# Three units of each up projection taken in two halves of 128 rows

## What is computed

```python
# first block
h = rmsnorm(x, norm_gains[l, 2]) * (1.0 + sc2) + sh2
y = jnp.square(jax.nn.relu(h @ w1[l] + b1[l])) @ w2[l] + b2[l]     # w1: 1024 x 4096
x = x + g2 * rmsnorm(y, norm_gains[l, 3])
# second block
h = h + _swiglu(_rms_norm(h, norm_ffn_g[l]), w_ffn_in[l], w_ffn_out[l])   # w_ffn_in: 1024 x 5632
def _swiglu(x, w_in, w_out):
    g, u = jnp.split(x @ w_in, 2, axis=-1)
    return (jax.nn.silu(g) * u) @ w_out
```

## Time and profile before

| | |
|---|---|
| median of three runs | 787.77 us |
| the profiled execution | 789.94 us |
| its span, first to last instruction | 788.2 us |
| TensorE busy | 734.8 us, 93% |
| VectorE busy | 517.8 us, 66% |
| ScalarE busy | 450.2 us, 57% |
| mean granted clock of TensorE | 0.974 of full |

### The profile page before, as it was taken

One profiled execution on the slowest core, in us unless ns is written; L12 is line 12 of the kernel. 1 busy time (PEld: TensorE's weight loads), 2 busy tenths in 40 slices (PEclk: granted clock), 3 DMA queues, 4 the chain that ended last, 5 costly groups with the idle time before them and its releaser, 6 DMA issues.

```text
span 788.2 us, 12072 instructions
## 1 busy us (share of the span) xinstructions
PE 734.8 (93%) x4062; PEld 619.8 (79%) x4062; DVE 517.8 (66%) x764; ACT 450.2 (57%) x724; POOL 44.4 (6%) x77
## 2 busy tenths in 40 slices
PE   0599999789999999989999999999897999999998
PEld 0498966589999886767989777777686888888886
DVE  6877697777877643457657465665747777777443
ACT  1654678666666433355455687554446777777331
POOL 3100100100000100014101000000000000000000
PEclk9899999979999999998999999999997999999999
DMA  8999985257787655534763564544444666656661
GB/s 315 368 330 338 262 278 167 81 150 206 233 240 263 213 187 166 175 117 115 227 189 114 181 187 131 164 125 138 148 123 134 179 188 175 201 175 197 203 196 57
DMA packets 137167, 150.50 MB, mean 191 GB/s; under 512 B 6164, under 2 KB 111783, under 8 KB 137129
## 3 DMA queue, kind: packets, MB, share of 16 engines
q1 hardware_dynamic: 135278, 145.28, 59.9%
q10 hardware_dynamic: 1852, 4.75, 1.7%
HBM read 148.57 MB, written 1.44 MB: 190 GB/s over the span
## 4 chain that ended last, share of the span: by engine, by line
PE 80%; DVE 10%; issue 4%; ACT 3%; DMA 3%; POOL 1%; SPq 0%; POOLq 0%; DVEq 0%; ACTq 0%
PE acc L1363 13%; PE acc L1364 13%; PE acc L1365 13%; PE acc L1355 11%; PE acc L1342 6%; PE acc L1344 6%; PE acc L1343 6%; PE acc L1356 5%; DVE ada_sum L1038 3%; DMA raw<-in_w_ada 2%; PE aux L1331 2%; DVE wl L960 1%; DMA raw<-in_w_out 1%; PE acc L1595 1%; ACT wh L594 1%
## 5 line engine op out<-in xcount | busy, mean ns | idle before, releaser
L960 DVE TENSOR_TENSOR wl<-raw,wh 128x1024 fp32r<-128x1024 f32 x217 | 266.2, 1232 | 149.5 <-ACT wh L594 148.4
L594 ACT ACTIVATE wh<-raw 128x1024 fp32r<-128x1024 f32 x217 | 227.9, 1055 | 125.6 <-PE acc L1365 109.6
L1342 PE MATMUL acc<-xT,wh 128*128 128x256 f32 x440 | 126.9, 288 | 5.5 <-DVE xT L990 4.1
L1355 PE MATMUL acc<-xT,wh 128*128 128x512 f32 x352 | 127.0, 405 | 0.8 <-DVE xT L982 0.8
L1344 PE MATMUL acc<-xT,wl 128*128 128x256 f32 x440 | 126.1, 287 | 0.0
L1343 PE MATMUL acc<-xT,wh 128*128 128x256 f32 x440 | 126.1, 287 | 0.0
L1363 PE MATMUL acc<-wh,xT 128*128 128x512 f32 (+1 forms) x272 | 111.0, 408 | 4.7 <-DVE xT L982 2.6
L1364 PE MATMUL acc<-wl,xT 128*128 128x512 f32 (+1 forms) x272 | 106.5, 391 | 0.0
L1365 PE MATMUL acc<-wh,xT 128*128 128x512 f32 (+1 forms) x272 | 106.3, 391 | 0.0
L1356 PE MATMUL acc<-xT,wl 128*128 128x256 f32 x352 | 100.0, 284 | 0.0
L1342 PEld LDWEIGHTS acc<-xT,wh 128*128 128x128 f32 x440 | 85.9, 195 | 7.5 <-issue 5.9
(11 more groups left out here) (260 smaller groups left out, 877.1 us busy)
## 6 DMA issues: line engine op xcount, KB each, us to landing
raw<-in_w_in SPq DMA_DIRECT2D x66, 512.0 KB, 3.6
raw<-in_w SPq DMA_DIRECT2D x64, 512.0 KB, 3.8
raw<-in_w_ffn_in SPq DMA_DIRECT2D x44, 512.0 KB, 4.1
raw<-in_w_ada SPq DMA_DIRECT2D x27, 512.0 KB, 6.5
raw<-in_w_ffn_out SPq DMA_DIRECT2D x22, 512.0 KB, 4.3
raw_more<-in_w_ada SPq DMA_DIRECT2D x13, 512.0 KB, 7.2
raw<-in_w_out SPq DMA_DIRECT2D x13, 512.0 KB, 4.8
rows_tmp<-in_w_ada ACTq DMA_DIRECT2D x8, 512.0 KB
```

What stands on the lines that cost most here:

```text
L594: A(wh[:, s, :], raw_unit, ACT.Copy).then_inc(rounded, 1)
L960: V.tensor_tensor(wl[:, s, :], raw_slot(r), wh[:, s, :].bitcast(f32), ALU.subtract).then_inc(split_ready, 1)
L1342: mm(bank[:, 0:ROWS], wh[:, s, w], hi, start=(kt == 0), stop=False)
L1355: mm(bank[:, :], wh[:, s, w], moving[:, kt, :], start=(kt == 0), stop=False, skip_group_check=True)
```

## The change

In both up projections the first three units are no longer taken by the loop but written out in parts. A new function `row_part` multiplies one unit by one row tile (128 rows) for some of the kt. TensorE's new order in up 1: transposes of row tile 0; units 0 and 1 by row tile 0, kt 0 to 3; unit 0 by row tile 0, kt 4 to 7; transposes of row tile 1; unit 1 by row tile 0, kt 4 to 7; unit 2 by row tile 0; then units 0, 1 and 2 by row tile 1; then the fourth unit as before, and the loop from its second pass on, without waits for columns. In up 2 units 0 and 1 by row tile 0, kt 0 to 3 stand ahead of the transposes of row tile 1 and kt 4 to 7 of both behind them. In up 1 a part has three matmuls over 128 columns for each kt; in up 2 one over 256 (the high and the low part of 128 rows) and one over 128. ScalarE and VectorE get their steps in an order that fits.

```diff
@@ ScalarE, up 1
             square_rows(N_FF1, 1)
+            from_transposed(X_UP1, 0, range(4, KT), A2, sh2)
             round_static(U_UP1 + 2)
-            from_transposed(X_UP1, 0, range(4, KT), A2, sh2)
             from_transposed(X_UP1, 1, range(KT), A2, sh2)
@@ VectorE, up 1
             split_columns(X_UP1, 0, range(4), 4)
             low_static(U_UP1 + 1)
+            split_columns(X_UP1, 0, range(4, KT), 4)
             normalise(N_FF1, 1)
-            split_columns(X_UP1, 0, range(4, KT), 4)
+            low_static(U_UP1 + 2)
             split_columns(X_UP1, 1, range(KT), 2)
-            low_static(U_UP1 + 2)
@@ VectorE, up 2
             split_columns(X_UP2, 0, range(4), 4)
+            low_static(U_UP2 + 1)
             normalise(N_FF2, 1)
             split_columns(X_UP2, 0, range(4, KT), 4)
-            split_columns(X_UP2, 1, range(4), 2)
-            low_static(U_UP2 + 1)
-            split_columns(X_UP2, 1, range(4, KT), 2)
             low_static(U_UP2 + 2)
+            split_columns(X_UP2, 1, range(KT), 2)
@@ TensorE
+            def row_part(u, t, r, kts, bank, both):
+
+                s = slot_of(u)
+                pe.wait_ge(split_ready, u + 1)
+                for kt in kts:
+                    pe.wait_ge(xT_ready, X_COUNT * t + (4 * (kt // 4 + 1) if r == 0 else KT + 2 * (kt // 2) + 2))
+                    w, rows = slice(P * kt, P * (kt + 1)), slice(P * r, P * (r + 1))
+                    moving = xT[:, kt, :].rearrange("p (c n) -> p c n", c=2)[:, :, rows]
+                    first, last = kt == 0, kt == KT - 1
+                    if both:
+                        out = bank[:, :].rearrange("p (c n) -> p c n", c=2)[:, :, rows]
+                        mm(out, wh[:, s, w], moving, start=first, stop=False, skip_group_check=True)
+                    else:
+                        mm(bank[:, rows], wh[:, s, w], moving[:, 0, :], start=first, stop=False, skip_group_check=True)
+                        mm(bank[:, rows], wh[:, s, w], moving[:, 1, :], start=False, stop=False, skip_group_check=True)
+                    ins = mm(bank[:, rows], wl[:, s, w], moving[:, 0, :], start=False, stop=last, skip_group_check=True)
+                return ins
@@ TensorE, up 1
-            for r in range(RT):
-                to_columns(xr, r, X_UP1, normed, RT + r + 1)
-
+            to_columns(xr, 0, X_UP1, normed, RT + 1)
+            pe.wait_ge(resid, 1)
+            for k in range(2):
+                row_part(U_UP1 + k, X_UP1, 0, range(4), acc[k], False)
+            row_part(U_UP1, X_UP1, 0, range(4, KT), acc[0], False)
+            to_columns(xr, 1, X_UP1, normed, RT + 2)
+            row_part(U_UP1 + 1, X_UP1, 0, range(4, KT), acc[1], False)
             pe.wait_ge(resid, RT)
-            with pe.Fori(0, D_FF // P // RING) as i:
+            row_part(U_UP1 + 2, X_UP1, 0, range(KT), acc[2], False)
+            for k in range(3):
+                row_part(U_UP1 + k, X_UP1, 1, range(KT), acc[k], False).then_inc(unit_done, 1)
+            col_unit(U_UP1 + 3, U_UP1 + 4, acc[3], xT)
+            with pe.Fori(1, D_FF // P // RING) as i:
                 for k in range(RING):
                     pe.wait_ge(acc_free, F_PROJ1 - RING + k + 1 + RING * i)
-                    col_unit(U_UP1 + k, U_UP1 + k + 1 + RING * i, acc[k], xT, columns_ready(X_UP1) if k == 0 else None)
+                    col_unit(U_UP1 + k, U_UP1 + k + 1 + RING * i, acc[k], xT)
@@ TensorE, up 2
+            pe.wait_ge(resid, 2 * RT + 1)
+            for k in range(2):
+                row_part(U_UP2 + k, X_UP2, 0, range(4), acc[k], True)
             to_columns(xr, 1, X_UP2, normed, 3 * RT + 2)
+            for k in range(2):
+                row_part(U_UP2 + k, X_UP2, 0, range(4, KT), acc[k], True)
             pe.wait_ge(resid, 3 * RT)
-            with pe.Fori(0, FF2 // P // 2) as i:
+            row_part(U_UP2 + 2, X_UP2, 0, range(KT), acc[2], True)
+            for k in range(3):
+                row_part(U_UP2 + k, X_UP2, 1, range(KT), acc[k], True).then_inc(unit_done, 1)
+            both_unit(U_UP2 + 3, U_UP2 + 4, acc[3], xT)
+            with pe.Fori(1, FF2 // P // 2) as i:
```

More of the change, by code:

```diff
@@ L1749, in _ @@
             wide_rows(U_OUT2, lambda k: xT[:, k, :], range(KT - 1, KT), 1, None, KT - 1)
+            pe.wait_ge(resid, 2 * RT + 1)
+            for k in range(2):
+                row_part(U_UP2 + k, X_UP2, 0, range(4), acc[k], True)
             to_columns(xr, 1, X_UP2, normed, 3 * RT + 2)
+            for k in range(2):
+                row_part(U_UP2 + k, X_UP2, 0, range(4, KT), acc[k], True)
             pe.wait_ge(resid, 3 * RT)
-            with pe.Fori(0, FF2 // P // 2) as i:
+            row_part(U_UP2 + 2, X_UP2, 0, range(KT), acc[2], True)
[3 more added lines that the diff above has]
+            with pe.Fori(1, FF2 // P // 2) as i:
                 for k in range(RING):
                     pe.wait_ge(acc_free, F_PROJ2 - RING + k + 1 + RING * i)
-                    both_unit(U_UP2 + k, U_UP2 + k + 1 + RING * i, acc[k], xT, columns_ready(X_UP2) if k == 0 else None)
+                    both_unit(U_UP2 + k, U_UP2 + k + 1 + RING * i, acc[k], xT)
             n_hid = FF2 // P
```

## The result

The changed kernel takes 803.02 us (median of 8 runs) against 788.03 for the kernel before beside it (8 runs). The comparison gives a ratio of 1.0117, interval 1.0076 to 1.0158: slower by 1.2%. (The comparison leaves out the two longest executions, 805.97 and 805.28, as disturbed, but both belong to the upper of the two groups described next, so its ratio is too low; the quotient of the medians is 1.019.) The forecast was 805.7, with slower at 0.64.

The account below looks back on a forecast made before the run. TensorE, busy 93% of the span, was taken as the bound, with hand-over gaps carried whole to the end. Up 1 +18.4 and up 2 -0.5 gave +17.9: 807.8 profiled, 805.7 in the runs' terms, range 786 to 813.

Parts of the forecast that it names:

- The narrow matmul costs a whole one: Divided units: a matmul on 128 columns takes 0.112 us at full clock, 0.213 at low, paced by its weight load.
- The second rival: 128 columns cost half of 256, by the page's issue gap: up 1 -5.6, up 2 -5.8, total 776.4; chance 0.04.
- Up 1, +16.35 and +2.05: Up 1 at low clock throughout: fourth unit starts 16.35 us late, then loses 2.05 itself; sum +18.4.
- A clock that stays low through all 144: Up 1: the clock falls and does not rise under the 144 narrow matmuls; forecast case, chance 0.55.
- The first rival: The clock rises also under loads that fill the time: up 1 +2.9, up 2 -2.4, total 788.3; chance 0.33.
- The transposes in the middle: Rival: row tile 1's transposes bring the clock back half way through up 1, about +8, 795 to 799; chance 0.08.
- The edits costed at nothing: Semaphore waits, VectorE's later normalise of row tile 1 and the low parts of units 2 and 3: zero for all.
- Up 2, -0.5: Up 2 divided: 2.6 us more work against an earlier start, ending at 608.7 against 609.16; -0.5.
- (c): Up 2: the clock falls and eight gap-free transposes bring it back near 600; end 608.7, -0.5; the case taken.
- case (a): Up 2: the clock doesn't fall; end at 605.8 against 609.16, -3.4.
- The sum: Whole kernel: +18.4 - 0.5 = +17.9, so 807.8 in the profiled execution's terms and 805.7 in the runs'.

Follow-up runs that it names:

- the split transposes: The changed kernel with the eight transposes of row tile 1 before up 1 in two groups of four, 24 narrow matmuls between: 804.38 to 807.69, ratio 1.0203.
- the repeat: The changed kernel run again without an edit, six executions: median 798.89, ratio 1.0101.
- the fillers: The changed kernel with 14 unread matmuls of 512 columns in TensorE's idle time before up 1's first part: 788.19 beside 788.88, ratio 0.9996.

## Why the prediction came out as it did

**The narrow matmul costs a whole one.** Right. I took 0.112 at full clock from the earlier trace rows, and 0.213 at the low one from bounds of 0.112 and 0.224. Measured 0.112 and 0.213. The second rival (half the columns, half the cost) is out: with the clock up, 144 of them and eight transposes needed 17.1 us (158.59 to 175.72), where it would have given half of that.

**Up 1, +16.35 and +2.05.** The first is the measured 16.35 of an upper execution to the last digit. Part of that is luck: I had the first part starting 5.78 us after the last matmul before, and it was 5.91; the other terms made up for it. The second was too large: the fourth unit lost 1.4. The clock was back after 3.0 us there, and I had taken 4.1, the length of the low clock in the unit of before; and I had counted half of it as lost, where steps of 0.213 instead of 0.120 lose 44%. The 3.0 isn't fixed: with the split transposes the fourth unit began at 189.58 and the clock was back 4.9 us later.

**A clock that stays low through all 144.** Right in eight executions of 14, wrong in six. The first rival, a rise under loads that fill the time, was in none of the traces: 35 us of narrow matmuls and eight transposes without a gap, and 0.50 all along.

**The transposes in the middle.** Here the working failed. I had read from the earlier trace rows that transposes alone bring the clock back, and used that in up 2. The rows leave out eight more between the two groups, also slow, so that 24 slow ones and not sixteen stand ahead of the rise there:

```profile
28.54 1.92 PE L1331 MATMUL acc<-ident,ada_sum 128*128 128x128 f32 x8
```

In up 1 the same eight gap-free transposes stand, and there I gave it 0.08 and priced it at +8. They did it in six of 14 executions. Its price, +8 or 795 to 799, was wrong as well: I counted the low clock for half of the matmuls, but the transposes stand behind the first 36 of 144. By the steps of the prediction itself, 108 matmuls at 0.112 instead of 0.213 are 10.9 us less, and the fourth unit's 2.05 falls away: 805.7 - 13.0 = 792.7. The lower group lies at 793. I should have set the two as nearly equal, and given both times.

What decides between them isn't shown. Up to the end of the transposes an upper and a lower execution have the same steps, but not at the same distance from the fall of the clock. In the lower one it fell at 156.6 and the transposes began at 164.95; in the two upper ones it fell at 156.8 and 156.6, and they began at 166.71 and 166.45. The later start comes from the attention stage, where the low clock lasted until 105.4 in the lower one and until 109.1 and 108.8 in the others. That is one trace against two. The Trainium skill (TensorE: Matmul & The Clock Gate, Part 1) says that the count of slow matmuls at a kernel's start differs from run to run, with the phase of the chip's own count. These runs agree in kind: the same code of up 1 finds its clock back at 166.8 or at 194.4. On transposes the same page of the Trainium skill (Part 4) says that they don't count as busy time for the clock in the same way; the durations beside it are of bf16, and these transposes are float32. The measurements decide against it here: the rise at 170.0 fell among transposes of which 16 had been added for nothing but that, and with them the upper group was gone.

**The edits costed at nothing.** Semaphore waits, the later normalise and the low parts in up 1: nothing of them shows. TensorE has no gap from the first part to the fourth unit, save the 2.0 us of 37 that lie ahead of 159.00. The transposes of row tile 1 stood behind 36 matmuls, as assumed.

**Up 2, -0.5.** Of the three cases I took the clock that falls and comes back (c); in this execution it didn't fall (case (a)). Of the eight profiles with up 2 divided and no filler ahead of it, five are like this one, and three show (c): low for 3.4 us and back 0.3 to 1.2 us behind the transposes, with hand-overs of 16.10 to 16.40. So (c) was a real case, but I had sized it at 17.6, with a clock low for 6.9 us. The kernel before had 3.68 us idle there in one piece; now 2.0 and 0.34 are left, and in up 1, with 1.87 and 2.59 idle around the first transposes, the clock fell in every trace without fillers. I had no row for an idle time as short as 2.0 in this place. Case (a) was worked out as -3.4 and gave -2.61: the transposes start at 614.66 and not when four more pairs are through, since VectorE writes the second unit's low part before it normalises row tile 1, and TensorE waits 0.34 for that. And of the 2.61, 0.9 is what this one profile of before had more than another undivided execution (17.10).

**The sum.** 807.8 was worked out for the profiled execution and it took 805.97. By terms: up 1 0.0, fourth unit -0.6, up 2 -2.1, and +0.8 (1.72 - 0.9) from stretches of unchanged code whose clock differs from one execution to the next. That the median, 803.02, lies close to 805.7 is luck as well: five of the eight executions fell in the upper group, and in the repeat, with three of six, the median was 798.89.

## What to carry to other kernels

To start a product early on part of its rows, look at what one matmul is bound by. Where each has its own 128 x 128 load, 128 columns cost 0.112 us and 256 cost 0.120, and in up 1 the head start of 5.6 us was paid back in full before anything was gained. Then look at the clock that the early part runs at. A short idle gap followed by narrow work held the low level for 35 us here, where wide work ended it in 3 to 6 (3.0 and 4.9 in two fourth units of up 1, 6.1 in the second projection of before). What gained most here was to put wide matmuls that nobody reads into the gap: 784.66 instead of 788.59, with no other edit, and it gives something only where the operands are ready for a faster engine. And where a kernel's times fall into two groups, look at the clock in a profile of each before taking a median.

## What the runs showed of the hardware

- Transposes in float32 brought TensorE's clock back: judged by the times, eight without a gap in six executions of 14 (and two of four with up 1 alone divided), 24 in six of six, two groups of four in none of four. A trace each shows the rise at 166.8, right behind eight, and at 170.0, among 24.
- Narrow matmuls (128 columns, a 128 x 128 load each) didn't bring it back in 35 us without a gap (eight transposes among them), but keep it once it is up (17 us at 1.00 with the fillers).
- The same divided code of up 2 keeps the clock in five profiles (hand-over 15.4) and loses it for 3.4 us in three (16.1 to 16.4).
- At the low level such a matmul takes 0.213 us and at the full one 0.112, so the pace of a matmul bound by its load follows the clock. A pair of 256 and 128 columns takes 0.43 and 0.23, hardly more than two narrow ones.
- The moment at which the clock comes back is worth 11 us in one hand-over: the same program runs at 793 or 804 us, on the same chip, with nothing between.
